# One stage for output product, second norm and query product of a hybrid layer step

## What is computed

```python
mod = jax.nn.silu(c) @ w_ada + b_ada
sh1, sc1, gt1, sh2, sc2, gt2 = [m[:, None, :] for m in jnp.split(mod, 6, axis=-1)]
h = rms_norm(x, g_pre_mix) * (1 + sc1) + sh1
...
mix = (jax.nn.sigmoid(zga) * y_a + jax.nn.sigmoid(zgb) * y_b) @ w_out
x = x + gt1 * rms_norm(mix, g_post_mix)
h2 = rms_norm(x, g_pre_ffn) * (1 + sc2) + sh2
f = peer(h2, w_pq, k_sub1, k_sub2, u_exp, v_exp)
x = x + gt2 * rms_norm(f, g_post_ffn)
```

## Time and profile before

| | us |
|---|---|
| median of 3 runs (6190.89 to 6213.27) | 6201.21 |
| the profiled execution | 6202.39 |
| its span | 6200.8 |
| last matmul of "mo" issued | 2840.56 |
| first matmul of "pq" | 3077.56 |

### The profile page before, as it was taken

The page is one execution under the profiler, slowest core; times in us unless marked ns, Lnnn a source line. Parts: engine busy times, 40 slices in busy tenths (PEclk is TensorE's granted clock), DMA queues, the critical chain, the costliest instruction groups (busy, mean ns, idle before and its releaser), DMA issues. The chain is left out here.

```text
span 6200.8 us, 63131 instructions
## 1 busy us (share of the span) xinstructions
PE 5121.9 (83%) x22772; PEld 4059.5 (65%) x22772; DVE 3599.7 (58%) x3976; ACT 1575.2 (25%) x1858; POOL 2129.5 (34%) x1576
## 2 busy tenths in 40 slices
PE   6879999999978879896693109999999788888885
PEld 2337888888866337684382109999999566666664
DVE  5642211126662333212312957887777799999998
ACT  5643121222221111121110103332222232232222
POOL 0100000000001330000000676888888655555553
PEclk9999999999989989896596559999999899999998
DMA  8752332233323544321324229999999999999997
GB/s 301 264 176 86 104 100 90 91 104 114 109 87 138 190 167 163 122 93 69 118 93 187 21 19 397 380 389 371 378 373 383 369 393 392 393 399 392 394 392 291
DMA packets 462792, 1409.59 MB, mean 227 GB/s; under 512 B 98220, under 2 KB 188249, under 8 KB 377579
## 3 DMA queue, kind: packets, MB, share of 16 engines
q1 hardware_dynamic: 279902, 731.78, 32.8%
q0 software_dynamic: 155712, 635.75, 27.8%
q10 hardware_dynamic: 27072, 40.91, 1.9%
HBM read 1264.87 MB, written 144.49 MB: 227 GB/s over the span
## 5 line engine op out<-in xcount | busy, mean ns | idle before, releaser
L219 DVE TENSOR_TENSOR w_lo<-w_stage,w_hi 128x2048 fp32r<-128x2048 f32 x248 | 569.0, 2294 | 1471.9 <-ACT w_hi L215 1457.5
L224 PE MATMUL ps<-w_hi,act_hi 128*128 128x512 f32 x3040 | 1196.4, 394 | 45.8 <-DVE act_lo L1109 23.0
L225 PE MATMUL ps<-w_lo,act_hi 128*128 128x512 f32 x3040 | 1191.3, 392 | 0.0
L226 PE MATMUL ps<-w_hi,act_lo 128*128 128x512 f32 x3040 | 1191.0, 392 | 0.0
L1545 POOL DMA_INDIRECT d_wT<-wt_all,put_all x384 | 766.3, 1996 | 290.7 <-DVEq L1660 137.1
L215 ACT ACTIVATE w_hi<-w_stage 128x2048 fp32r<-128x2048 f32 x248 | 474.6, 1915 | 1524.3 <-PE ps L226 1419.3
L2000 DVE SCALAR_TENSOR_TENSOR acc<-v_ring,coef,acc 128x2048 f32<-128x2048 f32 x254 | 802.8, 3161 | 50.6 <-DMA v_ring<-v_exp,idx_all 37.0
L1880 PE MATMUL ps<-act_hi,x_hi 128*128 128x384 f32 x2048 | 694.1, 339 | 150.6 <-DVE x_lo L2005 148.2
L1880 PE MATMUL ps<-x_hi,cx_hi 128*128 128x512 f32 x1536 | 618.1, 402 | 216.3 <-DVE cx_lo L2010 176.7
L1952 ACT ACTIVATE x_hi<-x_stage 128x1024 fp32r<-128x1024 f32 x512 | 540.9, 1056 | 934.0 <-DMA x_stage<-u_turned 526.2
L2005 DVE TENSOR_TENSOR x_lo<-x_stage,x_hi 128x1024 fp32r<-128x1024 f32 x512 | 623.8, 1218 | 159.2 <-ACT x_hi L1952 159.1
(11 more groups left out here) (258 smaller groups left out, 5535.5 us busy)
## 6 DMA issues: line engine op xcount, KB each, us to landing
x_stage<-u_turned SPq DMA_DIRECT2D x256, 512.0 KB, 7.5
x_stage<-v_exp SPq DMA_DIRECT2D x256, 512.0 KB, 8.6
w_stage<-w_ada SPq DMA_DIRECT2D x96, 1024.0 KB, 4.8
w_stage<-w_in SPq DMA_DIRECT2D x96, 1024.0 KB, 5.2
gw<-d_g SPq DMA_DIRECT2D x256, 192.0 KB, 7.4
gw<-d_wT SPq DMA_DIRECT2D x256, 192.0 KB, 10.7
d_wT<-zero SPq DMA_DIRECT2D x12, 2048.0 KB, 28.3
d_g<-gob ACTq DMA_DIRECT2D x128, 192.0 KB
```

The costliest lines, as they stand in the source:

```text
L219: dve.tensor_tensor(w_lo[:, q % 2], w_in_st[:, q], w_hi[:, q % 2].bitcast(F32), ALU.subtract).then_inc(w_split, 1)
L224: pe.matmul(out, lhs[0], rhs[0], start=first, stop=False)
L225: pe.matmul(out, lhs[0], rhs[1], start=False, stop=False)
L226: return pe.matmul(out, lhs[1], rhs[0], start=False, stop=last)
```

## The change

The three stages "mo", "n2" and "pq" become one, `mid_stage`, written without hardware loops. "yo" loads and splits the first quarters of `w_out` before it ends (`then`). The sums of the output product are not stored: ScalarE takes the sum of squares of each bank, VectorE multiplies the bank by `gate * g_post_mix`, spread over the partitions by DMA, into `x2` in SBUF. After the last chunk VectorE scales and adds x in one pass for each tile; the second norm then runs as the first stage's does, on turned rows. The query product begins when four of the 16 turned blocks are split. Rows of `h2` are made and stored for tiles 3 and 4 alone, between the quarters of the first query chunk; `experts` reads no others. The first stage makes the products of conditioning and norm rows on nine partitions (four passes in place of one) and turns the second norm's rows into `d_mod2t`. `route` no longer makes and stores `d_post`.

```diff
     d_mod = dram("d_mod", (NSEQ, 6 * D))
+    d_mod2t = dram("d_mod2t", (P, 2 * KD * 10))
...
-    d_post = dram("d_post", (NSEQ, D))
+    d_post = d_mod[:, 5 * D:6 * D]
...
+        SCALE0, TURN0, MT, AFF0, POST1, SCALE2 = 7, 8, 10, 14, 12, 20
...
+            pool.wait_ge(gain_done, 1)
+            pool.dma_start(g9[:], a["g_post_mix"].broadcast_to([NSEQ, D])).then_inc(s_g9, 16)
...
-            pool.wait_ge(mod_read, NA)
+            for n, name in ((1, "g_pre_ffn"), (2, "g_post_ffn")):
+                pool.wait_ge(gain_done, n + 1)
+                pool.dma_start(g9[:], a[name].broadcast_to([NSEQ, D])).then_inc(s_g9, 16)
+            pool.wait_ge(m2_taken, 1)
+            pool.dma_start(d_mod2t, mod_t[:].rearrange("p m k s -> p (m k s)")).then_inc(s_modout, 16)
+            pool.wait_ge(gain_done, 4)
             pool.dma_start(d_mod, mod[:]).then_inc(s_modout, 16)
-            pool.wait_ge(s_modout, 16)
+            pool.wait_ge(s_modout, 32)
...
+                if c == POST1 or c == NA - 1:
+                    n, at = (1, 2 * D) if c == POST1 else (3, 5 * D)
+                    dve.wait_ge(s_g9, 16 * (n + 1))
+                    dve.wait_ge(mod_read, c + 1)
+                    dve.tensor_tensor(mod[:, at:at + D], mod[:, at:at + D], g9[:], ALU.mult).then_inc(gain_done, 1)
+                if c == SCALE2:
+                    dve.wait_ge(s_g9, 48)
+                    dve.wait_ge(mod_read, c + 1)
+                    dve.scalar_tensor_tensor(out=mod[:, 4 * D:5 * D], in0=mod[:, 4 * D:5 * D], scalar=1.0, in1=g9[:],
+                                             op0=ALU.add, op1=ALU.mult).then_inc(gain_done, 1)
+                if c == NA - 1:
+                    dve.wait_ge(m2_ready, 1)
+                    dve.wait_ge(h_prompt, KD)
+                    dve.wait_ge(h_sample, 2 * KD)
+                    dve.tensor_copy(mod_t[:].rearrange("p m k s -> p (m k s)"), ps[:, 3, 0:2 * KD * 10]
...
+                if c == SCALE2 + 1:
+                    pe.wait_ge(gain_done, 3)
+                    pe.wait_ge(m2_clear, 1)
+                    for m in range(2 * KD):
+                        mm = pe.transpose(ps[:, 3, 10 * m:10 * m + NSEQ], mod[:, 3 * D + m * P:3 * D + (m + 1) * P],
+                                          kc[0:NSEQ, K_ID:K_ID + NSEQ])
+                    mm.then_inc(m2_ready, 1)
...
-    def norm_stage(name, src, col_shift, col_scale, g_row, G0, credit, residual=None):
...
+            xt = nc.alloc_sbuf_tensor_at("mid_x", [P, 4, NCOL], F32, offset=room)
+            xres = nc.alloc_sbuf_tensor_at("mid_res", [P, D], F32, offset=room)
+            postc = nc.alloc_sbuf_tensor_at("mid_post", [P, 2, NCOL], F32, offset=room + 16 * NCOL)
+            ob = nc.alloc_sbuf_tensor_at("mid_ob", [P, TT, NCOL], F32, offset=room)
+            x2 = sb(st, "mid_x2", [P, TT, D])
...
+                for t in range(TT):
+                    for g in range(4):
+                        sp.wait_ge(t_taken, t * 4 + (G0 + g + 1))
+                        sp.dma_start(xt[:, g], d_m[t * P:(t + 1) * P, g * NCOL:(g + 1) * NCOL]).then_inc(s_x[g], 16)
+                    if t == 0:
+                        sp.dma_start(m2t[:].rearrange("p m k s -> p (m k s)"), d_mod2t).then_inc(s_m2t, 16)
+                for i in range(n_ch):
+                    if i > 0:
+                        for q in range(QPC):
+                            load_quarter(sp, c_m + i, q, rows(a["w_out"], i * NCOL, q))
+                        sp.wait_ge(bank_free, (g_m + i + 1) * TT)
+                    at = slice(2 * D + i * NCOL, 2 * D + (i + 1) * NCOL)
+                    sp.dma_start(postc[:, 0], d_mod[0:1, at].broadcast_to([P, NCOL])).then_inc(post_in, 16)
+                    for j in range(STREAMS):
+                        sp.dma_start(postc[j * ST_TOK:(j + 1) * ST_TOK, 1],
+                                     d_mod[1 + j:2 + j, at].broadcast_to([ST_TOK, NCOL])).then_inc(post_in, 16)
+                sp.wait_ge(t_taken, G0 + 4 * TT + 4)
+                sp.dma_start(xres[:], a["x"][0:P, :]).then_inc(x_in, 16)
+                for q in range(QPC):
+                    load_quarter(sp, c_p, q, rows(a["w_pq"], 0, q))
+                for t in range(1, TT):
+                    sp.wait_ge(x2_done, t)
+                    sp.dma_start(xres[:], a["x"][t * P:(t + 1) * P, :]).then_inc(x_in, 16)
+                for i in range(1, n_ch):
+                    for q in range(QPC):
+                        load_quarter(sp, c_p + i, q, rows(a["w_pq"], i * NCOL, q))
...
+                for t in range(TT):
+                    pool.wait_ge(x2_done, t + 1)
+                    pool.dma_start(d_x2[t * P:(t + 1) * P, :], x2[:, t]).then_inc(x2_kept, 16)
+                pool.wait_ge(s_m2t, 16)
+                pool.wait_ge(nt_taken, 4 * TT)
...
+                pool.wait_ge(x2_kept, 16 * TT)
+                pool.wait_ge(scaled, TT)
+                for i, t in enumerate((TP - 1, TP)):
+                    for m, at in enumerate((4 * D, 3 * D)):
+                        pool.wait_ge(rows_used, 2 * i + m)
+                        row_load(0, i, at)
+                    pool.wait_ge(row_h, i + 1)
+                    pool.dma_start(d_h2[t * P:(t + 1) * P, :], x2[:, t]).then_inc(h_kept, 16)
+                for i in range(n_ch):
...
+                for t in range(TT):
+                    pe.wait_ge(scaled, t + 1)
+                    for g in range(4):
+                        if t > 0:
+                            pe.wait_ge(nt_taken, 4 * (t - 1) + g + 1)
+                        for j in range(4):
+                            mm = pe.transpose(ps[:, 4 + g, j * P:(j + 1) * P],
+                                              rows2[:, t, (4 * g + j) * P:(4 * g + j + 1) * P], ident)
+                        mm.then_inc(nt_ready, 1)
+
+                def h_there(q):
+                    pe.wait_ge(h_lo, 4 * q + 4)
+
+                h_there(0)
+                multiply_chunk(pe, c_p, g_p, between=lambda q: h_there(min(q + 1, QPC - 1)))
+                for i in range(1, n_ch):
+                    multiply_chunk(pe, c_p + i, g_p + i)
+
...
+                for i in range(n_ch):
+                    for q in range(1, QPC):
+                        split_hi(act, c_m + i, q, (g_m + i) * TT + acc_base)
+                    split_hi(act, c_m + i + 1, 0, acc_base)
+                    for t in range(TT):
+                        act.wait_ge(acc_done, (g_m + i) * TT + acc_base + t + 1)
+                        if i + t > 0:
+                            act.wait_ge(mo_sq, i * TT + t)
+                        act.activation(ps[:, 7], ps[:, t], ACT.Square, accum_out=sqs[:, t, i:i + 1]).then_inc(mo_sq, 1)
...
+                for t in range(TT):
+                    act.wait_ge(x2_done, t + 1)
+                    act.activation(turned2[:, t].rearrange("p k n -> p (k n)"), x2[:, t], ACT.Square,
+                                   accum_out=ns[:, 3, t:t + 1]).then_inc(v2_sq, 1)
+                act.wait_ge(v2_var, 1)
+                act.activation(ns[:, 5], ns[:, 4], ACT.Sqrt).then_inc(v2_std, 1)
+                act.wait_ge(v2_rstd, 1)
+                for t in range(TT):
+                    act.activation(rows2[:, t], x2[:, t], ACT.Copy, scale=ns[:, 6, t:t + 1]).then_inc(scaled, 1)
+                act.wait_ge(s_m2t, 16)
+                act.wait_ge(nt_taken, 4 * TT)
+                for k in range(KD):
+                    act.activation(turned2[:, 0:TP, k], turned2[:, 0:TP, k], ACT.Identity, scale=m2t[:, 1, k, 0:1],
+                                   bias=m2t[:, 0, k, 0:1]).then_inc(h_prompt, 1)
+                    if k > 0:
+                        act.wait_ge(h_prompt, k)
+                        act.wait_ge(h_sample, 2 * k)
+                        act.activation(act_hi[:, :, k - 1], turned2[:, :, k - 1], ACT.Copy).then_inc(h_hi, 1)
+                act.wait_ge(h_prompt, KD)
+                act.wait_ge(h_sample, 2 * KD)
+                act.activation(act_hi[:, :, KD - 1], turned2[:, :, KD - 1], ACT.Copy).then_inc(h_hi, 1)
...
+                    dve.wait_ge(post_in, (i + 1) * 16 * (1 + STREAMS))
+                    for t in range(TT):
+                        dve.wait_ge(acc_done, (g_m + i) * TT + (acc_base + t + 1))
+                        dve.wait_ge(mo_sq, i * TT + t + 1)
+                        dve.tensor_tensor(x2[:, t, i * NCOL:(i + 1) * NCOL], ps[:, t], postc[:, t // TP],
+                                          ALU.mult).then_inc(bank_free, 1)
...
+                dve.tensor_reduce(ns[:, 7], sqs[:], AX.X, ALU.add).then_inc(v1_sum, 1)
...
+                for t in range(TT):
+                    dve.wait_ge(x_in, 16 * t + 16)
+                    dve.scalar_tensor_tensor(out=x2[:, t], in0=x2[:, t], scalar=ns[:, 2, t:t + 1], in1=xres[:],
+                                             op0=ALU.mult, op1=ALU.add).then_inc(x2_done, 1)
+                dve.wait_ge(v2_sq, TT)
...
+                for t in range(TT):
+                    for g in range(4):
```

(34 more changed lines are left out.)

256 lines of the change are left out of this document (116 added, 140 removed).

## The result

The changed kernel takes **6039.67 us**, the median of four runs (6025.84 to 6053.19), against 6207.24 (6190.89 to 6216.88) for the kernel before, run beside it. The ratio is 0.9733, with a 95% interval of 0.9696 to 0.9769: 2.7% faster. In a second comparison, beside later experiments, it took 6037.3 (four runs) and its ratio was 0.9728 (0.9701 to 0.9756). The forecast was 6040, with a range of 6018 to 6068.

What follows compares the result with a forecast made beforehand. Products were taken as bound by TensorE, the norm between them by its own serial chain. Terms -10.9 - 167.4 + 8 + 8.8 = -161.5 took the profiled 6202.4 to 6040.9, stated as 6040 us; range 6018 to 6068.

Steps and rivals of the forecast that it cites:

- Start of the output product: Output product's beginning: d_m rows issued ahead of the weight quarters bring the first turned group 10.9 us earlier; bounds 8, 12.
- The output product itself: Output product's banks: the new square on ScalarE and multiply on VectorE hide beside TensorE; 0 us.
- E to query product: Last output matmul's end to first query matmul: the serial norm falls from 236.6 to 69.2 us, gaining 167.4.
- the rounds of x: Five passes adding x from one buffer: pass, handoff and load repeat every 8.5 us, between 7.4 and 11.6; 36.3 in all.
- First query chunk: Query product's start: ScalarE finishes 16 blocks before splitting the second quarter, so TensorE waits; +8 us, bounds 3 and 14.
- the stall: After the first query quarter: TensorE waits 6.3 us for the second quarter's split.
- First stage: Conditioning stage: added passes, transposes and work behind the last chunk lengthen VectorE's path; +8.8 us, bounds 6 and 12.
- Two passes (chunks 12 and 20) at 2.3, the nearest to its own duration: First stage on VectorE: each added pass priced at 2.3 us, from a range of 2.3 to 3.3.
- Routing and experts, 0: Later stages: the removed routing pass and store lie under 24 MB of zeros, and experts stays as it was; 0 us.
- GpSimd and VectorE in each other's way: Second norm's blocks: GpSimd operations wait out VectorE subtractions, costing 14 us, time 6054; chance 0.12.
- The early rows don't help: Output product's start: d_m rows land late for another reason, a cold queue; 10.9 us lost, time 6051; chance 0.05.
- Straight-line code starves TensorE: Both products: matmuls without loops slow down from instruction fetch; 6232 us at 0.1 more each; chance 0.02.

Runs made afterwards that it cites:

- weights_first: Changed kernel with the output product's first four weight quarters loaded and split ahead of the d_m rows again, as before the change; 6057.98 us in one run.
- first_bare: Changed kernel without three added first-stage passes, the 32 further transposes with their copy, and norm-row loads; 353.2 us from second sum to next stage.

## Why the prediction was right

The sum was -161.5 us; the two profiles of the first comparison show -163.5 up to the start of the experts (3712.1 to 3548.6). The rest of the 173.6 by which their spans differ lies in the experts (2488.7 and 2478.6), where thirteen profiles spread from 2461 to 2499 around the same code: the forecast of 0 there stands. That the median came within 1 us of 6040 is luck: errors of 2 to 4 us in three terms cancel, and the experts alone spread by 37. (The range is also looser in its making than it looks: the bounds given for its parts add up to 27 below and 39 above, or to 16 and 28 without the spread of runs, not to 22 and 28.) Term by term:

- **Start of the output product, -10.9.** Measured -11.0 (262.8 to 251.8), and 10.6 when it was undone. Right, and by the mechanism named, the rows behind 4 MB of weights.
- **The output product itself, 0.** The new squares and multiplies are hidden: ScalarE waits 2.03 us for TensorE before the last tile's square.
- **E to query product, -167.4.** Measured -170.1. Of its parts: to the first pass 3.7, measured 2.4 (2844.26 - 2841.83): square and multiply took 1.5, near the 1.6 forecast, but the reduce, mean, root and reciprocal 0.9 in place of 2.1, as the handoff of 0.27 stands there once and not at each; the rounds of x 8.5 each, measured 8.8; end of the last pass to the first transpose 5.9, measured 4.8 (2886.54 - 2881.74); transposes and copies 15.7, measured 14.7; four blocks 7.6, measured 7.1 (2908.34 - 2901.28). The round stood between 7.4 and 11.6 in the prediction; without the store it measured 7.0 to 7.4, so the lower bound was real, and the choice of 8.5, "near the lower end", was nearly right though its reason was not the whole of it: the store costs 1.5, not nothing.
- **First query chunk, +8.** Measured +5.8, but 3.8 of that lie in the product and 2.0 behind its last matmul. In the product the term that was too large is the stall: 6.3 forecast, 2.6 measured. A block takes ScalarE 1.33, not 1.43, which is 1.6 over sixteen, and the 1.5 added for GpSimd was not there. The cost of the clock was put at 1.7 and measured at some 1.5. The 2.0 are in no term of the prediction; the lines below this list show them.
- **First stage, +8.8.** The two profiles are 10.7 apart there, after 1.7 had gone the other way in the first two chunks, by their own spread; from the second sum on it is 12.4 (364.6 on average against 352.2). This is the term that was sized worst, just over its upper bound of 12. The step that failed is "Two passes (chunks 12 and 20) at 2.3, the nearest to its own duration": the rows gave 2.3 to 3.3 for the pass that was there, and the upper one was right: with that pass in pieces chunk 9 to 10 takes 15.8, where it took 19.11. The lower one came from an interval with 32 transposes in it, and these cost 2.0 (16.7 against 14.7), not 1.0. The runs show 3.5 for the pass of chunk 12 and some 5 for the pass of chunk 20 with the transposes, where 3.3 had been set. A pass does not cost its duration here, but what it does to the ring of `w_hi`, `w_lo` and products. The part behind the last chunk was put at 3.2 and measured 4.2: 3.4 up to the issue of the store of `mod`, and 0.9 more from that issue to the next stage, though the store lands in 9.3 us as it did in 9.2; no run takes that 0.9 apart. The term's error of 3.6 was covered by the 2.7 that E to query product gave more and the 2.2 that the first chunk took less, which is luck.
- **Routing and experts, 0.** From `zero` to `h_rows` 406.6 before and after.

What the prediction lacked: from the last matmul of the query product to `zero` it takes 9.3 us in all eleven profiles of the changed kernel and its edits, and 7.3 in both of the kernel before. The 2.0 lie in a drain instruction of GpSimd at the stage's end, behind which all engines wait at the barrier (before, then changed; durations in ns):

```profile
L140 POOLq DRAIN  x1: 1688/1688/1688, 3302.0 to 3302.0; - x1
```

```profile
L140 POOLq DRAIN  x1: 3727/3727/3727, 3136.4 to 3136.4; - x1
```

Why it is longer at the end of the new stage no run tells.

The rivals. *GpSimd and VectorE in each other's way*: the mechanism exists and its price on the path is 0: without the operations the blocks keep their pitch. The prediction's own counter-argument, the idle time of VectorE in each block, goes the right way (0.51 us idle of each 1.33). The Trainium skill ("GPSIMD Engine Reference", Key points) names the shared SBUF interfaces, and the trace agrees (0.40 alone, 0.89 to 1.03 in company); what it can't tell is which engine sets the pitch. *The early rows don't help*: fell with weights_first. *Straight-line code starves TensorE*: the median distance between the starts of two matmuls is 0.227 us in both products of the new stage, as before.

One more small thing is open. "yo", from its first load of `yo_x` to the next stage's first issue, takes 268.8 to 269.6 us in the profiles of the changed kernel and its edits, with the early weights and without them, and 271.2 in first_bare; in those of the kernel before it is 267.9 and 268.1. No run tells why.
